# Three of five sums of MLP halves, made by accumulating DMA in place of VectorE

## The reference

```python
h2 = rms_norm(x, norm_mlp_pre)
u = jax.nn.relu(h2 @ w_mlp_in)                          # 1024 -> 4096
x = x + rms_norm((u * u) @ w_mlp_out, norm_mlp_post)    # 4096 -> 1024
```

## Time and profile before

| | |
|---|---|
| median of three runs | 2730.1 us (2726.95 to 2731.36) |
| span of the profiled execution | 2728.4 us |
| TensorE busy | 2606.0 us, 96% of the span |
| VectorE busy | 1650.5 us, 60% |
| ScalarE busy | 1145.3 us, 42% |
| POOL busy | 162.5 us, 6% |

### The profile page before, as it was taken

One profiled execution on the slowest core, in us unless ns is written; L12 is line 12 of the kernel. 1 busy time (PEld: TensorE's weight loads), 2 busy tenths in 40 slices (PEclk: granted clock), 3 DMA queues, 4 the chain that ended last, 5 costly groups with the idle time before them and its releaser, 6 DMA issues. The chain is left out here.

```text
span 2728.4 us, 34994 instructions
## 1 busy us (share of the span) xinstructions
PE 2606.0 (96%) x14252; PEld 2056.3 (75%) x14252; DVE 1650.5 (60%) x2135; ACT 1145.3 (42%) x1686; POOL 162.5 (6%) x290
## 2 busy tenths in 40 slices
PE   7999999999999999989999999999999999998998
PEld 6867877666867766778888878878776788877777
DVE  4375443544344366955977767666567699843844
ACT  5472122343433445543454554444578522233131
POOL 0112110000100000100121100000000000000000
PEclk9999999999999999999999999999999999999999
DMA  4323321110323212651343488752111111113241
GB/s 159 116 89 64 56 52 55 54 44 20 112 69 105 66 39 90 217 194 70 126 159 140 147 299 307 246 212 78 68 42 54 57 60 55 53 49 144 69 170 47
DMA packets 104431, 289.74 MB, mean 106 GB/s; under 512 B 11224, under 2 KB 16120, under 8 KB 104272
## 3 DMA queue, kind: packets, MB, share of 16 engines
q1 hardware_dynamic: 80976, 208.01, 22.4%
q0 software_dynamic: 23296, 79.51, 9.1%
HBM read 225.54 MB, written 61.93 MB: 105 GB/s over the span
## 5 line engine op out<-in xcount | busy, mean ns | idle before, releaser
L281 PE MATMUL psum<-mixer_in,weights_parts 128*128 128x512 f32 x2016 | 475.8, 397 | 13.4 <-PEq L184 11.3
L281 PEld LDWEIGHTS psum<-mixer_in,weights_parts 128*128 128x128 f32 x2016 | 381.9, 190 | 108.0 <-issue 22.2
L453 PE MATMUL psum<-hidden,weights_parts 128*128 128x512 f32 x1536 | 403.6, 410 | 11.1 <-ACT early_gate L477 4.6
L453 PEld LDWEIGHTS psum<-hidden,weights_parts 128*128 128x128 f32 x1536 | 283.4, 191 | 86.6 <-issue 18.0
L248 DVE TENSOR_TENSOR weights_parts<-weights_raw,weights_parts 128x1024 fp32r<-128x1024 f32 (+2 forms) x110 | 107.5, 978 | 255.0 <-ACT weights_parts L232 254.9
L281 PE MATMUL psum<-hidden,weights_parts 128*128 128x512 f32 x1104 | 253.7, 392 | 5.5 <-PEq L878 2.8
L3427 PE MATMUL psum<-mixer_in,weights_parts 128*128 128x512 f32 x1104 | 255.5, 391 | 0.0
L3427 PE MATMUL psum<-mlp_in,weights_parts 128*128 128x512 f32 x1080 | 250.9, 392 | 1.9 <-DVE weights_parts L3279 1.7
L281 PEld LDWEIGHTS psum<-hidden,weights_parts 128*128 128x128 f32 x1104 | 207.0, 188 | 52.0 <-issue 6.9
L3427 PEld LDWEIGHTS psum<-mixer_in,weights_parts 128*128 128x128 f32 x1104 | 207.3, 188 | 45.4
L3427 PEld LDWEIGHTS psum<-mlp_in,weights_parts 128*128 128x128 f32 x1080 | 202.5, 188 | 47.5 <-DVE weights_parts L3279 3.4
(11 more groups left out here) (559 smaller groups left out, 4094.8 us busy)
## 6 DMA issues: line engine op xcount, KB each, us to landing
weights_raw<-in_w_in SPq DMA_DIRECT2D x69, 512.0 KB, 3.6
hidden_sums_scratch<-y POOLq DMA_DIRECT2D x84, 256.0 KB, 2.8
weights_raw<-in_w_gate SPq DMA_DIRECT2D x32, 512.0 KB, 3.7
gate_scratch<-early_gate SPq DMA_DIRECT2D x64, 256.0 KB, 2.1
gate<-gate_scratch POOLq DMA_DIRECT2D x32, 512.0 KB, 3.6
weights_raw<-in_w_mlp_back SPq DMA_DIRECT2D x30, 512.0 KB, 5.6
weights_raw_second<-in_w_mlp_back SPq DMA_DIRECT2D x30, 512.0 KB, 4.5
mod_weights<-in_mod_w POOLq DMA_DIRECT2D x48, 256.0 KB, 3.8
```

The source lines that it names most:

```text
L281: mm = nc.tensor.matmul(c.psum[:, bank + h, 0:cols], c.parts[:, s, wp, at], moving(k, xp, h), start=(n < halves), stop=(n >= halves * (3 * ...
L453: mm = nc.tensor.matmul(c.psum[:, bank, :], c.parts[:, s, wp, at], self.hidden[:, k, xp, h * HALF:(h + 1) * HALF], start=(k == 0 and n == ...
```

## The change

Of the five combinations three are sums (kinds 1, 6 and 7) and two are differences (3 and 4). VectorE makes the two differences only. For a sum POOL stores the first half into the place in DRAM, and later issues a second transfer of the other half to the same place that adds to what is there (`accum_op=ALU.add`). Between the two POOL waits until the five plain stores of the pair have landed. The three first halves go straight behind the two plain ones, the accumulating three behind the stores of the two differences. A pair's `pair_stored` counts eight transfers where it counted two, and those who waited for it wait for all eight: the copy on ScalarE into the rows, and SP's loads of combinations. The differences move on VectorE: to one each at places 2 and 3 for pair 0, and at places 5 and 6 of the next pair for the others; the sums at places 0 and 1 are gone.

```diff
--- before.py
+++ after.py
@@ -2850,16 +2850,24 @@
         sums_at = {0: (0, 2), 1: (4,), 2: (1,), 3: (0, 2), 4: (4,), 5: (1,), 6: (3,)}
         SUMS = ((1, (0, 0), (1, 1), 1), (3, (0, 1), (1, 1), -1), (4, (1, 0), (0, 0), -1),
                 (6, (0, 0), (0, 1), 1), (7, (1, 0), (1, 1), 1))
+        SUBTRACTED = [i for i, (*_, sign) in enumerate(SUMS) if sign < 0]
+        added_up = [(kind, halves) for kind, *halves, sign in SUMS if sign > 0]
+        stores_of = [2 + 2 * len(added_up) if pair < kept_pairs else 2
+                     for pair in range(HIDDEN_PAIRS)]
+
+        def stored_upto(pair):
+
+            return 16 * sum(stores_of[pair % 2:pair + 1:2])
 
         def sums_in(m):
 
             pair, k = into_at(m)
             if pair == first_pair and k < 5:
-                return [(0, i) for i in {2: (0, 1, 2), 3: (3, 4)}.get(k, ())]
-            of = pair - 1 if k >= 5 else pair - 2
+                return [(0, SUBTRACTED[k - 2])] if k in (2, 3) else []
+            of = pair - 1
             if of >= kept_pairs:
                 return []
-            return [(of, i) for i in {5: (0, 1), 6: (2,), 0: (3,), 1: (4,)}.get(k, ())]
+            return [(of, SUBTRACTED[k - 5])] if k >= 5 else []
 
         def evacuated_in(m):
 
@@ -2950,7 +2958,7 @@
         place_of = {kind: n for n, kind in enumerate(SEVEN)}
 
         def stored_sum(pair, i):
-            return 5 * pair + i
+            return len(SUBTRACTED) * pair + SUBTRACTED.index(i)
 
         def evacuated(eng, m):
 
@@ -3002,17 +3010,17 @@
                         if (pair, k) == (HIDDEN_PAIRS - 2, 0):
                             sp.wait_ge(pes.sem, pes.value(f"m{m - 1}"))
                             for n in range(2):
-                                sp.wait_ge(pair_stored[n], 16 * QUARTERS)
+                                sp.wait_ge(pair_stored[n], stored_upto(QUARTERS - 2 + n))
                             for n in range(4):
-                                sp.wait_ge(sum_stored[n], 16 * (5 * QUARTERS // 4))
+                                sp.wait_ge(sum_stored[n], 16 * (len(SUBTRACTED) * QUARTERS // 4))
                             load_quarter(0, 0)
                         if pair == HIDDEN_PAIRS - 1 and k in (1, 2):
                             sp.wait_ge(pes.sem, pes.value(f"m{m - 1}"))
                             if k == 1:
                                 for n in range(2):
-                                    sp.wait_ge(pair_stored[n], 16 * kept_pairs)
+                                    sp.wait_ge(pair_stored[n], stored_upto(kept_pairs - 2 + n))
                                 for n in range(4):
-                                    sp.wait_ge(sum_stored[n], 16 * (5 * kept_pairs // 4))
+                                    sp.wait_ge(sum_stored[n], 16 * (len(SUBTRACTED) * kept_pairs // 4))
                             load_quarter(0, k)
                     else:
                         turn, pair, third = back_at(m)
@@ -3026,7 +3034,7 @@
                         if turn == 6 and pair == 0 and third == 0:
                             sp.wait_ge(pes.sem, pes.value(f"m{m - 1}"))
                             for n in range(2):
-                                sp.wait_ge(pair_stored[n], 16 * HIDDEN_PAIRS)
+                                sp.wait_ge(pair_stored[n], stored_upto(HIDDEN_PAIRS - 2 + n))
                         for k in range(KT):
                             if m == back_place(6, 0, 0) + k:
                                 sp.dma_start(u_parts[:, k, 1, :].bitcast(F32),
@@ -3058,11 +3066,19 @@
                         pool.wait_ge(act.sem, act.value(f"square{pair}_{r}"))
                         pool.dma_start(t["hidden_sums"][place_of[kind]][pair],
                                        hidden_half(pair, r, r)).then_inc(stored, 16)
-                    for i, (kind, *_) in enumerate(SUMS):
-                        n = stored_sum(pair, i)
+                    for kind, ((r, half), _) in added_up:
+                        pool.dma_start(t["hidden_sums"][place_of[kind]][pair],
+                                       hidden_half(pair, r, half)).then_inc(stored, 16)
+                    for i in SUBTRACTED:
+                        kind, n = SUMS[i][0], stored_sum(pair, i)
                         pool.wait_ge(vecs.sem, vecs.value(f"sum{pair}_{i}"))
                         pool.dma_start(t["hidden_sums"][place_of[kind]][pair],
                                        ring[:, n % 4, :]).then_inc(sum_stored[n % 4], 16)
+                    pool.wait_ge(stored, stored_upto(pair) - 16 * len(added_up))
+                    for kind, (_, (r, half)) in added_up:
+                        pool.dma_start(t["hidden_sums"][place_of[kind]][pair],
+                                       hidden_half(pair, r, half),
+                                       accum_op=ALU.add).then_inc(stored, 16)
 
             @block.scalar
             def _(a):
@@ -3133,17 +3149,17 @@
                             pair = into_at(m)[0]
                             to = hidden_half(pair, r, half)
                             if n == 0 and kind == SEVEN[0]:
-                                a.wait_ge(pair_stored[pair % 2], 32 * (pair // 2))
+                                a.wait_ge(pair_stored[pair % 2], stored_upto(pair - 2))
                                 if pair - 2 < kept_pairs:
-                                    a.wait_ge(vecs.sem, vecs.value(f"sum{pair - 2}_4"))
+                                    a.wait_ge(vecs.sem, vecs.value(f"sum{pair - 2}_{SUBTRACTED[-1]}"))
                         else:
                             pair = back_at(m)[1]
                             to = back_half(pair, r, half)
                             if n == 0 and kind == SEVEN[0] and pair < 2:
-                                a.wait_ge(pair_stored[pair], 16 * HIDDEN_PAIRS)
+                                a.wait_ge(pair_stored[pair], stored_upto(HIDDEN_PAIRS - 2 + pair))
                             if n == 0 and kind == SEVEN[0] and pair == 2:
                                 for q in range(4):
-                                    a.wait_ge(sum_stored[q], 16 * (5 * kept_pairs // 4))
+                                    a.wait_ge(sum_stored[q], 16 * (len(SUBTRACTED) * kept_pairs // 4))
                         nc.scalar.activation(to, c.psum[:, bank(m), :], ACT.Copy,
                                              scale=sign).then_inc(act.step(f"copied{g}"), 1)
```

## The result

The changed kernel takes 2753.0 us (2749.2 to 2756.5, four runs) beside 2729.3 for the kernel before: a ratio of 1.0091, interval 1.0076 to 1.0105, so 23.7 us slower. The forecast was 5.7 us slower, with a range that ended at 2763. The sign and the place were right; the size was that of the second rival, build-up, and the range held it only because it reached as far as that rival.

What follows compares the result with a forecast made beforehand. TensorE was taken to bound the kernel, so VectorE's relief counted for nothing. The 2730.1 us median plus 5.7 at the first pair and 0 in later pairs gave 2735.8 us, range 2731.0 to 2763.0.

Steps and rivals of the forecast that it cites:

- second rival: In later pairs, accumulates landing after 5.3 us carry lateness from pair to pair; 6.4 to 33.4 us slower; chance 0.29.
- What bounds the kernel, and what is removed: MLP stretch: TensorE is always busy, so removing 24.6 us of VectorE sums gains half a microsecond at most.
- Who waits: ScalarE's copy two pairs later waits for all eight transfers; at the first pair TensorE loses L + 1.1, 5.7 us.
- The issue of an accumulate: On POOL, accumulating issues were taken to start 0.60 us apart, like plain ones, each issue taking 0.54 us.
- L: Time from issue to landing of a pair's third accumulate; taken as 4.6 us, between bounds 2.3 and 10.9.
- The doubled lone store: Landing of the third accumulate taken as twice a lone 2.3 us store, since DRAM is read before writing: 4.6 us.
- hidden, cost 0: Later pairs: the third accumulate lands 0.7 us before ScalarE's copy needs it, so nothing is lost up to L = 5.3.
- The law for the build-up: Eleven later pairs each add L - 5.3 of lateness; TensorE pays 11 x (L - 5.3) - 5.4 us, if positive.
- the formula: Whole cost: L + 1.1 + max(0, 11 x (L - 5.3) - 5.4), giving 5.7 us at L = 4.6.
- The case that I took for the most likely: Only the first pair's wait costs, with L from 3.0 to 5.3; 4.1 to 6.4 us slower; chance 0.48.
- The third rival: ScalarE's first-pair copy doesn't decide, leaving VectorE's relief alone; half a microsecond faster at most; chance 0.05.
- the first (like a store): Accumulates land like plain stores, L up to 3.0; 3.4 to 4.1 us slower, no difference that can be told; chance 0.18.

Runs made afterwards that it cites:

- e3: Changed kernel with a third place for a pair's rows, all accumulating transfers kept; 2731.0 us, ratio 1.0007 to the kernel before.
- e5: Kernel before with a third place for a pair's rows, all five sums on VectorE; 2728.6 us, ratio 0.9994 to the kernel before.
- e6: Changed kernel with one accumulating transfer a pair in place of three, the others left out; 2736.0 us, ratio 1.0031 to the kernel before.
- e8: Changed kernel with accumulating transfers of half the columns, the other half left out; 2728.0 us in one run, stage 6.7 us longer than before.
- e10: Changed kernel with pair 0's three accumulates issued before its two differences, a repeated run; 2748.6 us, ratio 1.0084 to the kernel before.
- e1: Changed kernel with each sum's second transfer a plain store in place of an accumulating one; 2737.1 us, ratio 1.0030 to the kernel before.

## Why the prediction was right, and where it was too small

**What bounds the kernel, and what is removed: right.** TensorE has no idle to give back, and e3 against e5 shows VectorE's 24.6 us at nothing.

**Who waits: right.** ScalarE's copy in front of product 6 of the stage, with no slack, and in the later pairs the same copy with a lead of 5.4 us in front of it.

**The issue of an accumulate: wrong.** "I take the same for an accumulating issue" took 0.60 us from one to the next; it is 0.9 (2.73 for three), and even a plain one follows after 0.53 (1.60 for three at 1512.89): the two stores of the earlier trace rows that gave the 0.60 had waited for VectorE in between. This adds 0.6 us to the third's issue.

**L: too small.** In the first pair the third went out near 1335.7 and had landed when ScalarE woke at 1342.1: 6.3 us, not 4.6. Together with the issue that is 5.7 + 0.6 + 1.7 = 8.0 us, and the stall was 7.9 (the start of product 6, 1344.49, against 1335.07 with the 1.5 us by which the changed kernel reached the stage later). The doubled lone store was right as a rule for one alone (4.0, e6); for the third of three it left out the two ahead of it, whose bytes count as well (with half of them the median landing falls from 5.7 to 3.8, e8). Alone an accumulate takes 4.0 - 2.3 = 1.7 us more than a store here. The prediction's estimate from the Trainium skill, page "Collectives: The Full Stack", section "The bandwidth ceiling: the fold count and why AG ≠ RS ≠ AR", 0.5 us for each accumulate above a store, has the right sign and is too small beside that. That page of the Trainium skill states its rule of the reduce step in a ring of cores, which nothing here is.

**The clock: not in the sum.** The first step lost 9.5 us, 1.6 more than the stall; it is told below.

**The later pairs: the step "hidden, cost 0" failed.** Its first half held: I had the accumulates go 6.24 us after the end of the squares, and they went 6.29 after. From there I had 1.2 + 4.6 to the third's landing and it took 1.8 + 5.6, which turns 0.7 us early into 0.9 late. The last copy that waits is this:

```profile
1568.69 1.08 ACT L3163 ACTIVATE y<-psum 128x512 f32<-128x512 f32 x2 [7.00 <-DMA hidden_sums_scratch<-y]
```

The law for the build-up held: the copy at 1357.90 is 2.6 us late (e10, above), and the ten that follow it up to 1568.69 stand 21.08 us apart in the mean, 1.85 too far; 2.6 + 18.5 less the lead of 5.4 is 15.7 us, and 16.0 were lost. The same sum for e10 (6.9 late, then ten copies up to 1562.32, 1.75 too far) gives 19.0, where 19.3 were lost. The pair shown above is 0.9 late. The mean is 1.85 because in other pairs the first halves land later (0.5 us later on average; POOL waits 3.4 us at the longest, not 1.8), and because the accumulates take longer, too (0.4 us on average; up to 8.6 us from the first issue to the copy, not 7.5). Put in terms of the formula, L was 7.15, which gives 23.2 us: my second rival, to which I gave 0.29. Its signs, waits in every pair and pairs longer than 19.2 us, both came. The case that I took for the most likely, a cost at the first pair alone, did not.

**The third rival** (faster) and the first (like a store) fell: e1 shows that the first would have cost 5.6 us, more than the 3.4 to 4.1 that I gave it, and 1.4 of that is the clock's.

## What to carry to other kernels

Before work is moved from an engine to a transfer, look at who frees the buffer. In this kernel VectorE freed a row at the end of its sum; a transfer frees it when it has landed, and two dependent transfers two landings later. If the buffer then turns over slower than the bound engine's period, each round adds to the lateness, and a small error in a latency is multiplied by the rounds; give the buffer one more place first (e3), or do not move the work. And relief for an engine that works beside the bound one can be worth nothing, as the 24.6 us of VectorE were here.

## What the hardware showed that was not expected

An accumulating transfer from POOL takes 0.88 us to issue alone and 0.9 each in a row, against 0.54; 256 KB land in 4.0 us alone and 5.7 in the median of threes, against 2.3 at best and 2.8 in the median for plain ones in the same place (e1).

A stall of TensorE can cost more than its length. When the matmuls start again after the 8.05 us of idle, the granted clock (as a share of 2.4 GHz) is 0.50, the 1.2 GHz level. It is 0.50 from 1343 to 1347 us and 1.00 from 1350 to 1353 (the changed kernel, columns as above):

```profile
1343.00:1345.00 2.00, 0.51 (x1) 0.50 (x2) 0.90 (x2) 2.00 (x5) 0.00 (x0) 0.50 0.31 127
1345.00:1347.00 2.00, 2.00 (x6) 1.53 (x5) 2.00 (x4) 0.48 (x2) 0.00 (x0) 0.50 0.73 215
1347.00:1350.00 3.00, 3.00 (x12) 2.38 (x12) 3.00 (x6) 0.86 (x2) 0.56 (x2) 0.82 0.76 296
1350.00:1353.00 3.00, 3.00 (x15) 2.46 (x14) 3.00 (x5) 1.18 (x2) 3.00 (x4) 1.00 0.64 133
```

The 36 matmuls behind it took 10.0 us (1344.49 to 1354.50) in place of the 8.46 of before (1335.08 to 1343.54), so 1.6 us more. The same fall followed the 1.8 us of idle before 1425.94 but not the 2.6 us before 1489.68:

```profile
1427.00:1429.00 2.00, 2.00 (x7) 1.51 (x6) 1.56 (x3) 2.00 (x5) 1.22 (x3) 0.50 0.77 260
...
1489.00:1491.00 2.00, 1.31 (x6) 1.10 (x7) 1.64 (x3) 2.00 (x4) 0.00 (x0) 1.00 0.30 43
```

What decides between them stays open; no run was made for it. The second fall made its 36 matmuls 1.7 us longer than the 8.24 of an undisturbed pair. Over the whole stage TensorE is busy for 257.9 us where it was 250.3 before, and the two falls are 3.3 of those 7.5 us; the rest stands in pairs with short gaps at a granted clock of 1.00, and no run shows what it is.
